# The first four units of a two-layer trunk kernel: two K tiles side by side, constants on SyncE's queue, the table's product earlier

## The reference

```python
h = rmsnorm(x, mix_norm[0])                 # x * rsqrt(mean(x^2) + eps) * gain
qkv = h @ w_qkv                             # 1024 x 1536, [512, 1024] @ it
bias = rel_bias[t5_bucket(rel)]             # a table of 32 buckets x 16 heads, spread over positions
scores = einsum(q, k_band) * 64**-0.5 + bias
```

## Time and profile before

| | |
|---|---|
| median of 3 runs | 1093.4 us |
| lowest and highest | 1091.97 and 1093.53 us |
| profiled execution | 1092.39 us, its span 1090.6 us |
| TensorE busy | 1069.8 us (98% of the span) |
| VectorE, ScalarE, GpSimd busy | 752.5, 492.7, 117.4 us |
| first matmul | 6.39 us after the span's start |

### The profile page before, as it was taken

One profiled execution on the slowest core, in us unless ns is written; L12 is line 12 of the kernel. 1 busy time (PEld: TensorE's weight loads), 2 busy tenths in 40 slices (PEclk: granted clock), 3 DMA queues, 4 the chain that ended last, 5 costly groups with the idle time before them and its releaser, 6 DMA issues.

```text
span 1090.6 us, 15616 instructions
## 1 busy us (share of the span) xinstructions
PE 1069.8 (98%) x5892; PEld 917.0 (84%) x5892; DVE 752.5 (69%) x1095; ACT 492.7 (45%) x763; POOL 117.4 (11%) x109
## 2 busy tenths in 40 slices
PE   7999999999999999999999999999999999999996
PEld 5888788888899888898788888888888899888896
DVE  5588657767876667787554556867676876667786
ACT  6366554434443334454752345454444433334452
POOL 3100030000100000123021221030000100000122
PEclk9999999999999999999999999999999999999998
DMA  6612032226642225552222211132226652225542
GB/s 196 163 58 78 6 131 97 96 96 183 160 137 102 97 97 170 140 158 70 88 78 91 84 40 58 60 114 97 96 96 183 159 157 99 97 97 169 132 122 90
DMA packets 43371, 121.10 MB, mean 111 GB/s; under 512 B 5202, under 2 KB 10098, under 8 KB 43316
## 3 DMA queue, kind: packets, MB, share of 16 engines
q1 hardware_dynamic: 34736, 106.45, 28.5%
q0 software_dynamic: 4608, 11.54, 6.3%
q10 hardware_dynamic: 3972, 2.38, 1.2%
HBM read 116.93 MB, written 2.88 MB: 110 GB/s over the span
## 4 chain that ended last, share of the span: by engine, by line
PE 92%; DVE 4%; ACT 2%; DMA 1%; issue 1%; SPq 0%; DVEq 0%
PE PS L464 68%; PE PS L522 18%; PE PS L637 1%; PE PS L655 1%; PE PS L645 1%; DVE XL L1317 1%; DMA X<-xT 1%; PE PS L775 1%; DVE X L1847 1%; PE PS L807 0%; PE PS L794 0%; DVE WL L1300 0%; PE PS L778 0%; PE PS L809 0%; PE PS L734 0%
## 5 line engine op out<-in xcount | busy, mean ns | idle before, releaser
L464 PE MATMUL PS<-XH,WH 128*128 128x512 f32 x992 | 392.8, 396 | 7.7 <-DVE XL L1317 7.6
L464 PE MATMUL PS<-XH,WL 128*128 128x512 f32 x992 | 387.3, 390 | 0.0
L464 PE MATMUL PS<-XL,WH 128*128 128x512 f32 x992 | 387.1, 390 | 0.0
L464 PEld LDWEIGHTS PS<-XH,WH 128*128 128x128 f32 x992 | 186.8, 188 | 49.6 <-issue 10.9
L464 PEld LDWEIGHTS PS<-XH,WL 128*128 128x128 f32 x992 | 186.8, 188 | 39.4
L464 PEld LDWEIGHTS PS<-XL,WH 128*128 128x128 f32 x992 | 187.0, 189 | 38.8 <-issue 1.0
L894 ACT CAST WH<-WRAW 128x1024 fp32r<-128x1024 f32 x137 | 142.6, 1044 | 167.3 <-DMA WRAW<-w_up 110.7
L1300 DVE TENSOR_TENSOR WL<-WRAW,WH 128x1024 fp32r<-128x1024 f32 x137 | 172.4, 1258 | 21.4 <-ACT WH L894 20.8
L1338 DVE TENSOR_TENSOR GS<-PS,R 128x512 f32<-128x512 f32 x44 | 30.4, 692 | 117.7 <-PE PS L464 117.7
L522 PE MATMUL PS<-AH,DH_Z 128*128 128x256 f32 x352 | 98.0, 278 | 0.6 <-DVE X L1433 0.3
L522 PE MATMUL PS<-AH,DL_Z 128*128 128x256 f32 x352 | 97.5, 277 | 0.0
(11 more groups left out here) (232 smaller groups left out, 1502.5 us busy)
## 6 DMA issues: line engine op xcount, KB each, us to landing
WRAW<-w_up SPq DMA_DIRECT2D x88, 512.0 KB, 3.2
WRAW<-w_bin SPq DMA_DIRECT2D x24, 512.0 KB, 3.2
DRAW_W<-w_down SPq DMA_DIRECT2D x24, 384.0 KB, 3.7
DRAW_W<-w_down SPq DMA_DIRECT2D x24, 320.0 KB, 3.0
WRAW<-w_qkv SPq DMA_DIRECT2D x11, 512.0 KB, 4.9
WSUM_Z<-w_down SPq DMA_DIRECT2D x12, 384.0 KB, 4.6
WSUM_Z<-w_down POOLq DMA_DIRECT2D x12, 384.0 KB, 6.4
WSUM_Z<-w_down SPq DMA_DIRECT2D x12, 320.0 KB, 3.8
```

The source lines that it names most:

```text
L464: last = mm(PS[:, bank], w[:, c:c + P], x[:, kb], start=start and n == 0 and w is wh and x is hi, stop=stop and n == len(kbs) - 1 and w is wl)
```

## The change

Eight things are edited, all in the first 45 us of the program:

- The first two K tiles (256 columns) of all four units are loaded, cast and subtracted ahead of their rests, and TensorE multiplies kb 0 of units 0 to 3, then kb 1 of units 0 to 3, then the rests unit by unit.
- The first piece of unit 0 is issued by ACT, the others by SP; `X` tile 0 becomes SP's first DMA.
- 14 float32 matmuls of ones with ones (128x128) into a bank not yet used stand ahead of everything on TensorE (`WARMING`).
- The table's product moves ahead of the rest of unit 0; ACT's copy of it and the DMA to `bias_rows` move to directly behind the eight casts of `X`.
- POOL copies only the first square (`POOL_SQUARES` 3 to 1); DVE adds the other seven, woven with the low parts of the rests.
- `mean_square` moves back in unit 2, from behind kb 3 to behind kb 6.
- The 14 constants' DMAs move from ACT (behind the cast of unit 5) to SP, behind the first four units' loads and ahead of the load of unit 4.
- ACT casts unit 4 ahead of `std(0)`, and DVE subtracts it ahead of the reciprocal; `lo_unit(5)` and `lo_unit(6)` stand behind the values' evacuation.

```diff
             sp.dma_start(X[:, 0], xT[:, 0]).then_inc(x_landed[0], 16)
+            for u in range(1, SLOTS):
+                load_first(u)
             sp.dma_start(X[:, 1], xT[:, 1]).then_inc(x_landed[1], 16)
-            sp.dma_start(WRAW[0][:, FIRST:D], w_qkv[0, :, FIRST:D]).then_inc(raw_landed[0], 16)
             sp.dma_start(X[:, 2:4], xT[:, 2:4]).then_inc(x_landed[2], 16)
+            load_rest(0)
             sp.dma_start(X[:, 4:6], xT[:, 4:6]).then_inc(x_landed[3], 16)
             sp.dma_start(X[:, 6:8], xT[:, 6:8]).then_inc(x_landed[4], 16)
-            for u in range(1, A_O):
+            for u in range(1, SLOTS):
+                load_rest(u)
+            sp.wait_ge(small_set, 1)
+            for dst, src in ((IDENT[:], ident), (CAUSAL[:], causal), (CAUSAL2[:], causal_pair),
...
+                sp.dma_start(dst, src).then_inc(consts, 16)
+            for u in range(SLOTS, A_O):
                 load(u, w_qkv[u])
...
+            pe.wait_ge(ones_set, 1)
+            for n in range(WARMING):
+                mm(PS[:, B7, 0:P], STD[:, 0:P], STD[:, 0:P], start=True, stop=True)
+            early = FIRST // P
+            for kb in range(early):
+                for u in range(SLOTS):
+                    pe.wait_ge(first_lo, u + 1)
+                    product(u, u, XH, XL, range(kb, kb + 1), kb, start=kb == 0, stop=False, part_ready=(xl_ready, 0))
             pe.wait_ge(rel_landed, 32)
             mm(PS[0:A_HEADS, B5, 0:REL], RB[0:32, :], HOT[0:32, :], start=True, stop=True).then_inc(tb_done, 1)
-            unit(1, 1, XH, XL)
-            pe.wait_ge(lo_ready, 3)
-            product(2, 2, XH, XL, range(0, 4), 0, stop=False)
+            rest(0, range(early, 8), part_ready=(xl_ready, 0)).then_inc(unit_done, 1)
+            rest(1, range(early, 8)).then_inc(unit_done, 1)
+            rest(2, range(early, 7), stop=False)
             pe.wait_ge(onesr_ready, 1)
             mean_square(0)
-            product(2, 2, XH, XL, range(4, 8), 4, start=False).then_inc(unit_done, 1)
-            unit(3, 3, XH, XL)
+            rest(2, range(7, 8)).then_inc(unit_done, 1)
+            rest(3, range(early, 8)).then_inc(unit_done, 1)
             unit(4, 0, XH, XL)
...
+            act.dma_start(WRAW[0][:, 0:FIRST], w_qkv[0, :, 0:FIRST]).then_inc(first_landed[0], 16)
             act.dma_start(GAIN[:], gains).then_inc(gain_landed, 16)
...
+            first_part(0)
+            act.wait_ge(gain_landed, 16)
+            first_x(0)
+            for u in range(1, SLOTS):
+                first_part(u)
+            for m in range(1, 4):
+                first_x(m)
+            x_square(0, 0)
+            rest_part(0)
+            first_x(4)
+            first_x(5)
+            x_square(0, 1)
+            first_x(6)
+            first_x(7)
+            act.wait_ge(tb_done, 1)
+            nc.scalar.copy(TB[0:A_HEADS, :], PS[0:A_HEADS, B5, 0:REL]).then_inc(tb_ready, 1)
+            act.wait_ge(tb_ready, 1)
+            act.dma_start(bias_rows.rearrange("h (q r) -> h q r", q=64),
+                          TB[0:A_HEADS, :].rearrange("h (o r) -> h o r", o=1).to_broadcast([A_HEADS, 64, REL]))\
+               .then_inc(rows_out, 16)
+            rest_part(1)
...
+            rest_part(3)
+            for m in range(5, KT_D):
                 x_square(0, m)
...
+            hi_unit(4)
             std(0)
-            hi_unit(4)
             hi_unit(5)
...
+            rest_part(1)
+            add_square(1)
+            add_square(2)
+            rest_part(2)
+            add_square(3)
+            rest_part(3)
+            for m in range(4, KT_D):
+                add_square(m)
+            lo_unit(4)
             inverse_rms(0)
```

More of the change, by code:

```diff
@@ L52 @@
 FIRST = 2 * P
-POOL_SQUARES = 3
+POOL_SQUARES = 1
 LANDED = {0: 0, 1: 1, 2: 2, 4: 3, 6: 4}
+WARMING = 14
 DVE_TILES = 6
@@ L250, in trunk @@
         unit_evac = sem("unit_evac")
-        first_landed, first_hi, first_lo = sem("first_landed"), sem("first_hi"), sem("first_lo")
+        first_landed = [sem(f"first_landed{u}") for u in range(SLOTS)]
+        first_hi, first_lo = sem("first_hi"), sem("first_lo")
         x_landed = [sem(f"x_landed{i}") for i in range(5)]
@@ L590, in down_phase, with rest @@
                 w12(n + 3)
[L593 to L597, removed]
+            def rest(u, kbs, **kw):
+                pe.wait_ge(lo_ready, u + 1)
+                return product(u, u, XH, XL, kbs, kbs[0], start=False, **kw)
+            pe.wait_ge(ones_set, 1)
[6 more added lines that the diff above has]
+                    product(u, u, XH, XL, range(kb, kb + 1), kb, start=kb == 0, stop=False, part_ready=(xl_ready, 0))
             pe.wait_ge(rel_landed, 32)
             mm(PS[0:A_HEADS, B5, 0:REL], RB[0:32, :], HOT[0:32, :], start=True, stop=True).then_inc(tb_done, 1)
-            unit(1, 1, XH, XL)
-            pe.wait_ge(lo_ready, 3)
-            product(2, 2, XH, XL, range(0, 4), 0, stop=False)
+            rest(0, range(early, 8), part_ready=(xl_ready, 0)).then_inc(unit_done, 1)
+            rest(1, range(early, 8)).then_inc(unit_done, 1)
+            rest(2, range(early, 7), stop=False)
             pe.wait_ge(onesr_ready, 1)
             mean_square(0)
-            product(2, 2, XH, XL, range(4, 8), 4, start=False).then_inc(unit_done, 1)
-            unit(3, 3, XH, XL)
+            rest(2, range(7, 8)).then_inc(unit_done, 1)
+            rest(3, range(early, 8)).then_inc(unit_done, 1)
             unit(4, 0, XH, XL)
@@ L1068, in _, with first_part, rest_part, first_x @@
             nc.scalar.copy(ONESR[:], STD[:, 0:P]).then_inc(onesr_ready, 1)
[L1069 to L1072, removed]
+            def first_part(u):
+                act.wait_ge(first_landed[u], 16)
+                nc.scalar.copy(WH[u][:, 0:FIRST], WRAW[u][:, 0:FIRST]).then_inc(first_hi, 1)
+            def rest_part(u):
+                act.wait_ge(raw_landed[u], 16)
+                nc.scalar.copy(WH[u][:, FIRST:D], WRAW[u][:, FIRST:D]).then_inc(hi_ready, 1)
+            def first_x(m):
                 if m in LANDED:
@@ L1075, in _ @@
                 x_hi(0, m)
[L1076 to L1082, removed]
-                x_square(0, m)
[L1084 to L1095, removed]
+            first_part(0)
@@ new lines, in _ @@
+            act.wait_ge(tb_ready, 1)
[3 more added lines that the diff above has]
+            rest_part(1)
+            x_square(0, 2)
+            rest_part(2)
+            x_square(0, 3)
+            x_square(0, 4)
+            rest_part(3)
+            for m in range(5, KT_D):
+                x_square(0, m)
+            hi_unit(4)
@@ L1602, in ffn, with first_part, rest_part, first_x @@
                     lo_unit(B_V + 2)
[L1604 to L1608, removed]
+            def first_part(u):
+                dve.wait_ge(first_hi, u + 1)
+                c = slice(0, FIRST)
+                tt(WL[u][:, c], WRAW[u][:, c], WH[u][:, c].bitcast(F32), ALU.subtract).then_inc(first_lo, 1)
+            def rest_part(u):
+                dve.wait_ge(hi_ready, u + 1)
+                c = slice(FIRST, D)
+                tt(WL[u][:, c], WRAW[u][:, c], WH[u][:, c].bitcast(F32), ALU.subtract).then_inc(lo_ready, 1)
+            def first_x(m):
                 if m in LANDED:
@@ L1611, in _, with add_square @@
                 x_lo(0, m)
[L1612 to L1618, removed]
+            def add_square(m):
                 dve.wait_ge(sq_ready, m + 1)
@@ L1621, in _ @@
                 tt(SS[:], SS[:], SQ[:, m % 2], ALU.add).then_inc(ss_ready, 1)
-            lo_unit(3)
+            first_part(0)
+            dve.wait_ge(gain_landed, 16)
+            first_x(0)
+            for u in range(1, SLOTS):
+                first_part(u)
+            for m in range(1, 4):
+                first_x(m)
+            rest_part(0)
+            for m in range(4, KT_D):
+                first_x(m)
+            rest_part(1)
+            add_square(1)
+            add_square(2)
+            rest_part(2)
+            add_square(3)
+            rest_part(3)
+            for m in range(4, KT_D):
+                add_square(m)
+            lo_unit(4)
             inverse_rms(0)
@@ L1631, in _ @@
                 last.then_inc(unit_evac, 1)
-                if t:
-                    lo_unit(4)
             for t in range(2):
@@ L1636, in _ @@
                 tt(VT[:, t], PS[:, 2 + t], R[:], ALU.mult).then_inc(unit_evac, 1)
+            for t in range(2):
                 lo_unit(5 + t)
```

11 lines of the change are left out of this document (10 added, 1 removed).

## The result

The changed kernel takes 1095.59 us (median of 11 runs, 1093.61 to 1097.49) against 1092.92 us (11 runs, 1090.79 to 1093.53): a ratio of 1.0026, 95% interval 1.0019 to 1.0034. It is **2.7 us slower**: the loss is small, but the interval lies wholly above 1. The forecast was a start of unit 4 0.4 us earlier, and a time of 1092.8 us.

A forecast was written before the change was run, and what follows sets the result against it. TensorE bounds the kernel, so unit 4's start decides: 33.8 + 0.2 = 34.0 us against 34.36, 0.4 us less. That gives 1092.0 from the profiled execution or 1093.0 from the median; forecast 1092.8, range 1090.0 to 1095.3.

The forecast's parts named there:

- The question: TensorE's start of unit 4, 34.36 us before: what follows was said to move by as much as this start.
- the step that decides: ScalarE: root behind unit 4's cast, whose load waits behind the table's DMA and lands at 25.9; unit 4 at 33.8 us.
- the forecast 30.6: TensorE's own end of unit 3, taken as 30.6 us, well ahead of 34.36.
- The rival by the Trainium skill: Unit 4's load interleaves with the table's DMA: start 31.3 or 32.1, gain 2.3 to 3.0 us, about 1090.2; chance 0.22.
- 33.8 + 0.2 = 34.0 us: Start of unit 4: 33.8 us by the late load plus 0.2 for the constants, 0.4 us less than 34.36.
- the choice to hold the clock: At unit 4: forecast case with start 33 to 34.8 us and no change of clock, chance 0.56.
- so 8.8 us again: ScalarE's wait for `X` tiles 2 and 3: 8.8 us as before, since 1024 KB stand ahead of them as before.
- So 14.3: ScalarE ahead of the table's copy: casts, squares and the rest's cast take 5.4 us from 8.8; DMA issued at 14.6.
- the same 11.3 us give its landing: Unit 4's load lands 11.3 us behind the issue of the table's DMA, as unit 5's did before: 25.9 us.
- The constants' 0.2: Constants' data on SyncE's queue ahead of unit 4's load: delay 0 to about 1 to 2 us, taken as 0.2.
- the second rival: Clock falls in TensorE's 3.4 us gap before unit 4: 1.2 to 2.6 us slower, about 1094.8; chance 0.14.
- That POOL drops two additions frees nothing that anyone waits for: Squares on DVE and POOL: dropping two of POOL's additions was said to gain nothing.

The follow-up runs named there:

- the kernel with the DMA in four: Changed kernel with the table's DMA cut in four DMAs of 16 copies each, one behind the other on ScalarE: ratio 1.0024.
- root first, filled: Changed kernel with the root ahead of unit 4's cast and nine products of ones in the gap ahead of unit 4: ratio 0.9990.
- the late table: Changed kernel with the table's copy and its DMA back behind the sixth square on ScalarE: ratio 0.9970.
- the filled gap: Changed kernel with 18 float32 products of ones between units 3 and 4: ratio 1.0013.
- the constants back: Changed kernel with the 14 constants' DMAs back on ScalarE behind the cast of unit 5: ratio 1.0023.
- root first: Changed kernel with the root ahead of unit 4's cast and unit 4's low part behind the first key evacuation: ratio 0.9991.
- before, with the products of ones: Kernel before the change with only the 14 products of ones put at its head: ratio 0.9995.
- POOL adds three squares: Table's DMA late and sum of squares behind kb 4, with GpSimd adding squares 1 and 2 again (`POOL_SQUARES = 3`): ratio 0.9972.
- the fastest kernel: Changed kernel with the table's copy and DMA late, and the sum of squares behind kb 4 of unit 2: ratio 0.9962.

## Why the prediction was wrong

**What held.** The question (when does unit 4 start), the step that decides (the cast of unit 4 ahead of the root, its load behind the table's DMA on another queue), and that two parts cost nothing at this start: the sum was whole at 25.2 us and asked for only at 26.1, and the constants' move changed nothing. TensorE ended unit 3 at 31.9 us, 1.3 later than the forecast 30.6, but still well ahead of unit 4. The rival by the Trainium skill ("DMA: Bandwidth & Descriptors", "Issuing engines are not separate DMA queues"), that the DMAs interleave, had 0.22 and fell: the trace has 10.2 us to landing, and the kernel with the DMA in four shows the size of what doesn't interleave. What the Trainium skill says in that page's section "Queues, rings and completion order", that a DMA engine drains a whole packet of one ring before it changes to another, fits it.

**The step that failed** is the sum's last: "33.8 + 0.2 = 34.0 us", measured 36.47, and with it the choice to hold the clock. The mechanism was right; two of its terms were too small, and the fall of the clock stood outside the sum. Its terms:

- "so 8.8 us again" for `X` tiles 2 and 3: 10.06 in this trace. Equal bytes ahead of a DMA do not make an equal landing; in the twelve profiled executions with this order of issue ScalarE cast them between 8.76 and 10.12 us, the middle at 9.5, and in the two with the old order at 8.81 and 8.82. That put the table's DMA at 15.86 in place of 14.6: **1.3 us**. ("So 14.3" is a slip, 8.8 and 5.4 are 14.2; it changes nothing.)
- "the same 11.3 us give its landing": 12.6 (15.86 to 28.4), **1.3 us** more. The load of unit 5, issued at 22.89, also waited, landed at 29.7, only 1.3 us behind that of unit 4, and by 28 us the bytes of both had moved (the windows above); that they share the turn is likely. But this doesn't settle why it is 12.6 and not 11.3: it is 12.5 to 12.6 in four traces with the early table and 11.6 in the fifth (root first, filled), where unit 5's load waited just the same, and 11.1 in that of the late table, where a second load, issued at 26.59, waited too. The cause stays open; what the trace does show is that one row, before's, was no bound for this term.
- The constants' 0.2: nothing that can be told (10.2 us to landing with them ahead of the load and without).

Together 36.3 to 36.5, against 34.0. And with the start moved by 2.5 us, and the end of unit 3 by 1.3, the gap was 4.5 in place of 3.4 us, so the second rival, **the fall of the clock**, given 0.14, came on top: 1.5 us in the trace, 1.4 by the filled gap. It was taken as an alternative to a late start, while both hang on the same number: a later start is a longer gap. The forecast gave this case "1.2 to 2.6 slower, about 1094.8"; 2.7 came. The range ended at 1095.3 since it took the fall of the clock with the start at 34.0 and not with the late one.

**The test that was missed**: the prediction itself had a new gap of 3.4 us and one trace to judge it by, and put six times as much weight on every other outcome. The traces show a fall at each gap of 4.3 to 4.5 us, and at gaps of 2.0 and 2.5 us; at those of 0.8 to 1.0 us none. The mean clocks of all runs add that it seems not certain even at 4.5 us: one of the changed kernel's 11 runs and two of the 12 with the constants back have 0.996 or more, as nearly all runs of before have.

**A reading that was wrong without harm here**: "That POOL drops two additions frees nothing that anyone waits for". In the trace of before, two low parts of `X` took VectorE 2.03 us and a low part of 1024 columns 1.91, beside GpSimd's additions, where they take 1.42 and 1.22 without. (Where VectorE's instruction had begun first, at 15.07 us, it took its 1.21 us, and GpSimd's addition took 2.17 in place of 1.38.) In the changed kernel unit 4 waits for the load, so it doesn't show.

## What to carry to other kernels

A long DMA can keep the loads of another queue waiting for its whole length (here 768 KB in rows of 768 bytes; that its length counts is shown, that the short rows do is not): before it is moved, ask which load will be issued while it runs and who waits for that one, and let nothing that everyone needs (here the root) stand in program order behind that wait. A gap on TensorE costs its length and then the slow matmuls behind it, so the lateness of a start and the fall of the clock belong in one case, not in two. Work that warms TensorE paid here only where no long wait followed it.

## What the runs showed of the hardware

- The 768 KB table's DMA lands 9.9 to 10.4 us behind its issue and moves 95 to 98 GB/s at 80% busy; a 512 KB load on the other queue, issued 1 to 2.6 us behind it, lands after 8.6 to 10.2 us, in place of 3.2 to 4.1 when it isn't in the way and 6.0 when it is cut in four.
- The granted clock fell right behind gaps of TensorE of 2.0 us (root first) and 2.5 us (before, with the products of ones), shorter than I had thought; at that of 2.0 us in five of 12 runs, by their mean clocks.
- VectorE's subtraction of 128x768 took 1.97 us beside an addition by GpSimd and 0.95 without one (POOL adds three squares; the fastest kernel).
- The landing of the same early loads differs by 1.4 us between executions of kernels with the same order of issue.
